# Value panels of a dilated attention as seven products for eight, and what moves with them

## The chip, the cores and the metric

The kernel runs on one core of a Trainium2 chip. The metric is device time in microseconds (us) of one execution, as the median of several runs. A core has five engines with their own instruction streams: TensorE (PE in the rows) multiplies matrices, VectorE (DVE) and ScalarE (ACT) work element by element, GpSimd (POOL) here adds weight blocks and starts transfers, SyncE (SP) starts transfers. They meet only at semaphores. Matrix products land in PSUM, eight banks of 128 x 512 f32; everything else lies in SBUF (in the rows: "arena").

## The reference

Two layers of a mixer (mLSTM branch, dilated attention branch, gates) and a swiglu MLP, then a windowed attention block and a gated linear attention block, for 256 tokens of width 1024, in f32. What the change touches is the value part of `qkv_a` and the order around it:

```python
def mixer(u, w_in, ...):
    z = u @ w_in
    qk_m, v_m, o_m, gate_m, qkv_a, gates_br = jnp.split(z, idx, axis=-1)
    y_a = mlstm_branch(qk_m, v_m, o_m, gate_m, ...) @ w_a
    y_b = dilated_attention(qkv_a, slopes) @ w_b
    g_a, g_b = jnp.split(gates_br, 2, axis=-1)
    return (jax.nn.sigmoid(g_a) * y_a + jax.nn.sigmoid(g_b) * y_b) @ w_out

def dilated_attention(qkv, slopes):          # three patterns, 8 slots, heads of 64
    ...
    for g, (win, dil) in enumerate(ATT_PATTERNS):
        o, lse = banded_attention(q[g], k[g], v[g], slopes[g], dil, win // (2 * dil))
    w = jax.nn.softmax(jnp.stack(lses, axis=0), axis=0)
    return (w[..., None] * jnp.stack(outs, axis=0)).sum(0)

# modulation, once a layer, from the vector c:
    ada = c_act @ w_ada[l] + b_ada[l]
    sh1, sc1, g1, sh2, sc2, g2 = jnp.split(ada, 6, axis=-1)
```

## The kernel before

The kernel is written by hand, engine by engine: one long function for TensorE, one for VectorE, one for ScalarE, one for GpSimd, each of which writes its instructions in the order in which they run. Semaphores order them across engines; a wait holds everything that stands behind it on that engine. The two layers run from 0 to about 640 us and on to about 1260 us, the two later blocks after that.

Weights come in panels of 512 columns (two panels make a group of 1024 x 512) into a ring of seven, loaded from SP. A layer's part that matters here runs so:

- Twelve query and key tiles ("AQK 0" to "AQK 11"), with pieces of the mLSTM between them, the minis. Behind some minis VectorE does a *modulation turn* (`beside_mix`): it multiplies one transferred part of `w_ada` by the vector c, with two scalar_tensor_tensor operations of 128x1028, or four where two vectors are to be served (a double turn; in layer 1 from its fifth turn on). The table `MINI_TURNS` says behind which minis. POOL starts the transfer for a later turn when a turn frees one of two slots.
- "HT 3", four transposes of the last mLSTM head, and then the value tiles "VA 0" to "VA 5", two for each of three patterns: 128 tokens x 512 columns, eight matmuls each. ScalarE copies them to SBUF.
- Scores, softmax, transposes and weighted sums of the dilated attention, by pairs of slots (`scores(u)`, `turned(u)`, `values(u)`, u = 0 to 3). A pair has two heads with two score tiles each: "SC 4 1" is head 4, tokens 128 to 255. VectorE drains both tiles of a head (with the distance bias), takes the row maximum and scales it, and goes on to the next head; ScalarE makes the exponentials; VectorE divides ("probs n").
- Between these, the gate products "GA p0", "GB p0", later "GA p1", "GB p1": a 1024-wide panel group times the tokens, made of seven products instead of eight. POOL makes two sums of weight blocks for each (`gate_weight_sums`), VectorE two more ("w6", "w3"), and the products are added up by VectorE from PSUM. They run in the order 1, 2, 4, 5, 7, 6, 3; product 6 needs w6.
- "WA 0", "WA 1", "WB 0", "WB 1", the output projections of both branches; VectorE multiplies each by its gate ("WB 0 drained"), adds ("mix 0"), and does turns between them, by the table in the loop. Then the second half with GA p1 and GB p1.

PSUM banks are taken in turn: `open_tile` hands out the next of eight, and the first matmul into it waits until its last tenant is drained. So the order of tiles decides whose drain a tile waits for.

In the rows one instruction of a helper has the helper's line: L598 and L600 are the transposes and matmuls, L2240, L2243 and L2246 VectorE's tensor_tensor, tensor_scalar and scalar_tensor_tensor, L2836 its maximum, L3455 and L3457 POOL's gate sums, L3439 and L3441 its sums for the MLP, L3470 and L3472 those of the last block, L3502 its transfers.

Of the kernel before, what the change touches and what calls it, by code (L numbers as in the profile page):

```python
# [265 lines left out]
def program(nc, a, out, marks):  # L266
    with ExitStack() as ctx:
# [19 lines left out]
        gate_sums_made = sem("gate_sums_made")  # L287
        mlp_sums_made = sem("mlp_sums_made")
# [222 lines left out]
        UP = [(name, p) for p in range(5) for name in ("W1", "W3")]  # L511

# [66 lines left out]
        def _(pe):  # L579
# [143 lines left out]
            for l in range(DEPTH):  # L723
# [86 lines left out]
                def va(j, w):  # L810

                    g, tt = j // 2, j % 2
                    ps = open_tile(f"VA {j}")
                    for i in range(KD):
                        x = UT[:, i, tt * P:tt * P + P]
                        if g:
                            x = by_residue(UT[:, i, :])[:, tt, :]
                        mm(ps[:, :PW], x, w[i][:, :PW], start=(i == 0), stop=(i == KD - 1),
                           done=f"VA {j}" if i == KD - 1 else None)

                def scores(u):
# [4 lines left out]
                    for tt in range(NT):  # L826
# [20 lines left out]
                def values(u):  # L847

                    if u == 0:
                        for j in range(6):  # L850
                            pe.wait_ge(act_done, AC.at(f"VA {j} drained"))
# [686 lines left out]
        def _(act):  # L1538
# [99 lines left out]
            for l in range(DEPTH):  # L1638
# [73 lines left out]
                def va(n):  # L1712

                    act.wait_ge(pe_done, PE.at(f"VA {n} full"))
                    drain(f"VA {n}", VA[:, n % 2, PW * (n // 2):PW * (n // 2) + PW]).then_inc(
                        act_done, AC.drained(f"VA {n}"))

                def exponentials_of(u):

                    for n in (2 * u, 2 * u + 1):  # L1720
# [40 lines left out]
                va(0)  # L1761
                exponentials_of(0)
                va(1)
                va(2)
                turned(0)
                exponentials_of(1)
                va(3)
                va(4)
                va(5)
# [465 lines left out]
        def _(dve):  # L2235
# [474 lines left out]
            for l in range(DEPTH):  # L2710
# [113 lines left out]
                token_sums("gates", up_x, [gate_tokens[i] for i in (5, 6, 4)], False, gate_tokens[7])  # L2824
                for u in range(SLOTS // 2):
                    for n in (2 * u, 2 * u + 1):
# [3 lines left out]
                        for tt in range(NT):  # L2830
# [8 lines left out]
                            dve_done, DV.step(f"slot negmax {n}"))  # L2839
                    for n in (2 * u, 2 * u + 1):  # L2840
# [3 lines left out]
                        for tt in range(NT):  # L2844
                            ts(SC[n % 2][:, tt, :], SC[n % 2][:, tt, :], att[:, n % 2, 3, tt:tt + 1], None, ALU.mult).then_inc(
                                dve_done, DV.step(f"probs {n}" if tt else None))
                    if u >= 2:
                        gate_panel(0, u - 2)
                    beside_mix(1)
                for p in range(2):  # L2850
# [11 lines left out]
                    for n in range(2):  # L2862
# [9 lines left out]
                        beside_mix(((0, 0, 0, 0), (1, 0, 0, 1))[l][j])  # L2872
# [547 lines left out]
        def _(pool):  # L3420
# [22 lines left out]
            def gate_weight_sums(l, p, b):  # L3443
# [133 lines left out]
```

## Time and profile before

| | us |
|---|---|
| median of 3 runs | 2267.65 (2266.7 to 2269.16) |
| profiled execution | 2266.64 |
| its span | 2264.8 |
| TensorE busy | 2229.2 (98%) |
| VectorE busy | 1430.7 (63%) |
| ScalarE busy | 488.7 (22%) |
| GpSimd busy | 287.4 (13%) |

The span is what the trace covers, from the first to the last instruction. A busy share is a mean over stages of different kinds; what a stage waits for is read in that stage. Each f32 matmul of the program is two rows in the trace, and a row's end is modelled, so the pace of TensorE is read from start to start. A turn of VectorE shows as scalar_tensor_tensor rows of 128x1028 with short accumulator reads between.

### The profile page before, as it was taken

Reading aid. Unit: us, or ns where it says so; the run is one execution under the profiler, and the core shown is the slowest. Engines: PE = TensorE matmul, PEld = TensorE weight load, DVE = VectorE, ACT = ScalarE, POOL = GpSimd, SP = SyncE. Lnnn points to the kernel's source line nnn. Section 1 sums busy time; section 2 is a strip of 40 time slices with the busy share of each in tenths; the row PEclk is TensorE's granted clock in tenths of the full one; section 3 lists DMA queues with packets and bytes.
Section 4 is the critical chain, followed back from the end, with each engine's and each line's share of the span. In section 5 each row is a group of like instructions: output and inputs, shape, how many; then the busy total and the mean of one; then the engine's idle time right before and its main releaser. Section 6 shows DMA issues by size and latency. Waiting matters only on the chain.

```text
span 2264.8 us, 30050 instructions
## 1 busy us (share of the span) xinstructions
PE 2229.2 (98%) x12022; PEld 1820.3 (80%) x12022; DVE 1430.7 (63%) x2592; ACT 488.7 (22%) x1067; POOL 287.4 (13%) x181
## 2 busy tenths in 40 slices
PE   7999999999999999999999999999999999999998
PEld 5888598799868885988998655588888887768987
DVE  5676453645656566756656777775576468766655
ACT  1212230110012223201010365422200023343300
POOL 0000121331000001223310000000000001001442
PEclk9999999999999999999999999999999999999999
DMA  9885546444576655465655411433433324445542
GB/s 393 295 315 190 190 164 220 170 154 168 198 279 188 230 186 205 172 219 196 185 196 177 168 38 39 158 113 130 154 132 124 121 94 168 131 168 186 179 166 84
DMA packets 179770, 398.77 MB, mean 176 GB/s; under 512 B 21168, under 2 KB 25648, under 8 KB 176560
## 3 DMA queue, kind: packets, MB, share of 16 engines
q1 hardware_dynamic: 136736, 285.03, 35.8%
q0 software_dynamic: 24080, 93.69, 12.0%
q10 hardware_dynamic: 18816, 18.12, 2.5%
q8 instruction: 97, 1.59, 0.3%
q14 instruction: 41, 0.34, 0.0%
HBM read 395.71 MB, written 1.11 MB: 175 GB/s over the span
## 4 chain that ended last, share of the span: by engine, by line
PE 94%; DVE 4%; ACT 1%; issue 0%; DMA 0%; POOL 0%; DVEq 0%; SPq 0%; ACTq 0%
PE bank L600 91%; PE bank L598 3%; DVE arena L2240 2%; DVE arena L2246 1%; ACT arena L1540 1%; DVE arena L2243 0%; DVE junk L2246 0%; DMA arena<-in_x 0%; ACT L1540 0%; ACT arena L1543 0%; DVE arena L2836 0%; POOL arena L3470 0%; POOL arena L3472 0%; DVE arena L3236 0%; DVE arena L2305 0%
## 5 line engine op out<-in xcount | busy, mean ns | idle before, releaser
L600 PE MATMUL bank<-arena 128*128 128x256 f32 (+4 forms) x11438 | 2169.1, 357 | 12.9 <-DVE arena L2246 3.7
L600 PEld LDWEIGHTS bank<-arena 128*128 128x128 f32 (+2 forms) x11438 | 1754.2, 189 | 407.3 <-issue 225.0
L2240 DVE TENSOR_TENSOR arena<-arena 128x1024 f32<-128x1024 f32 (+6 forms) x567 | 475.6, 854 | 206.1 <-PE bank L600 172.7
L1540 ACT ACTIVATE arena<-arena 128x512 f32<-128x512 f32 (+5 forms) x443 | 222.6, 525 | 796.5 <-DVE arena L2240 471.0
L2246 DVE SCALAR_TENSOR_TENSOR arena<-arena 128x1028 f32<-128x1028 f32 (+6 forms) x367 | 314.3, 873 | 83.2 <-DMA arena<-in_w_ada 60.3
L2240 DVE TENSOR_TENSOR arena<-arena,bank 128x256 f32<-128x256 f32 (+2 forms) x382 | 171.6, 474 | 185.0 <-PE bank L600 173.9
L3502 POOL DMA_DIRECT2D arena<-in_w_ada x88 | 62.9, 715 | 1447.5 <-DVEq L2255 1404.4
L1540 ACT ACTIVATE arena<-bank 128x256 f32<-128x256 f32 (+1 forms) x129 | 53.0, 429 | 558.5 <-PE bank L600 557.8
L2240 DVE TENSOR_TENSOR arena<-bank,arena 128x512 f32<-128x512 f32 (+2 forms) x95 | 60.4, 646 | 155.6 <-PE bank L600 140.4
L1543 ACT ACTIVATE arena<-bank 128x512 f32<-128x512 f32 (+1 forms) x163 | 88.5, 600 | 310.6 <-PE bank L600 272.4
L2246 DVE SCALAR_TENSOR_TENSOR arena<-bank,arena 128x254 f32<-128x254 f32 (+2 forms) x184 | 78.0, 468 | 57.9 <-PE bank L598 28.2
L2243 DVE TENSOR_SCALAR arena<-arena 128x512 f32<-128x512 f32 (+6 forms) x258 | 83.3, 352 | 20.1 <-ACT arena L1540 13.6
L598 PEld LDWEIGHTS bank<-arena 128*128 128x128 f32 x584 | 68.0, 143 | 27.2 <-issue 20.4
L598 PE MATMUL bank<-arena 128*128 128x128 f32 x584 | 74.6, 276 | 13.1 <-DVE arena L2243 11.1
L2246 DVE SCALAR_TENSOR_TENSOR junk<-arena 128x1028 bf16<-128x1028 f32 x64 | 79.7, 1245 | 5.7 <-DMA arena<-in_w_ada 1.5
L1540 ACT ACTIVATE arena<-bank,arena 128x128 f32<-128x128 f32 (+2 forms) x138 | 57.5, 484 | 99.9 <-DVE arena L2243 32.9
L3439 POOL TENSOR_TENSOR arena<-arena 128x1024 f32<-128x1024 f32 x20 | 49.3, 2466 | 180.2 <-DMA arena<-in_w 80.8
L2243 DVE TENSOR_SCALAR arena<-bank,arena 128x256 f32<-128x256 f32 (+1 forms) x112 | 46.3, 467 | 30.4 <-PE bank L598 14.1
L1540 ACT ACT_TABLE_LOAD x48 | 61.6, 1283 | 4.2 <-PE bank L600 2.2
L2246 DVE SCALAR_TENSOR_TENSOR arena<-arena,bank 128x512 f32<-128x512 f32 (+1 forms) x40 | 24.5, 643 | 43.5 <-PE bank L600 42.7
L3441 POOL TENSOR_TENSOR arena<-arena 128x1024 f32<-128x1024 f32 x20 | 51.2, 2562 | 1.6
L3470 POOL TENSOR_TENSOR arena<-arena 128x1024 f32<-128x1024 f32 x14 | 35.4, 2527 | 87.0 <-PE bank L600 73.1
(39 smaller groups left out, 260.5 us busy)
## 6 DMA issues: line engine op xcount, KB each, us to landing
arena<-in_w_ada POOLq DMA_DIRECT2D x88, 1028.0 KB, 5.8
arena<-in_w_in SPq DMA_DIRECT2D x84, 1024.0 KB, 7.6
arena<-in_w SPq DMA_DIRECT2D x56, 1024.0 KB, 6.9
arena<-in_w_mlp_in SPq DMA_DIRECT2D x32, 1024.0 KB, 7.3
arena<-in_w_mlp_out SPq DMA_DIRECT2D x32, 1024.0 KB, 6.9
arena<-in_w_gla SPq DMA_DIRECT2D x12, 1024.0 KB, 6.9
arena<-in_w_ada SPq DMA_DIRECT2D x16, 514.0 KB, 19.4
arena<-in_w_a SPq DMA_DIRECT2D x8, 1024.0 KB, 7.2
```

The costliest lines, as they stand in the source:

```text
L598: ins = nc.tensor.transpose(out, lhsT, rhs)
L600: ins = nc.tensor.matmul(out, lhsT, rhs, start=start, stop=stop)
L1540: return nc.scalar.activation(out, x, f, **kw)
L1543: return nc.scalar.activation(out, tile(key)[:, :out.free_size()], f)
L2240: return V.tensor_tensor(out, x, y, op)
L2243: return V.tensor_scalar(out, x, s1, s2, op0, op1) if op1 is not None else V.tensor_scalar(out, x, s1, None, op0)
L2246: return V.scalar_tensor_tensor(out=out, in0=x, scalar=s, in1=y, op0=op0, op1=op1, **kw)
L3439: nc.gpsimd.tensor_tensor(up_sum(at), a21, a22, ALU.add).then_inc(up_sums_made, 1)
L3441: nc.gpsimd.tensor_tensor(a21, a11, a21, ALU.subtract).then_inc(up_sums_made, 1)
L3470: nc.gpsimd.tensor_tensor(wsum, a21, a22, ALU.add).then_inc(mlp_sums_made, 1)
L3502: pool.dma_start(adaw[:, n % ADA_SLOTS], half_source(job, q)).then_inc(ada_in[n % ADA_SLOTS], 16)
```

## The change

The value tiles of a pattern become seven products of 512 x 256 blocks, like those of the gates: "VA g 1" to "VA g 7" for pattern g, each four matmuls (k = 0 to 3) of 256 columns. Pattern 0 uses the token sums that the gates have; patterns 1 and 2 use sums of strided tokens ("classes"), which VectorE makes once a layer. POOL makes two sums for each value panel (`value_panel_sums`), VectorE w6 and w3 and seven additions from PSUM, ScalarE one copy instead of two drains.

The order moves too. On TensorE the first two products of pattern 0 stand ahead of the scores of pair 0, four of pattern 1 ahead of `turned(0)` with its last three behind, product 3 of pattern 1 goes into a given bank; the first half of the scores of pair 2 stands ahead of `values(0)`, the second behind `turned(1)`. The modulation turns move from pairs 0 to 2 into the minis and to WB 0 (layer 0) and WB 1 (layer 1). POOL's first two gate sums wait for "probs 3" and "probs 5", and the later ones stand two jobs (GA p1) and one job (GB p1) later. The gates' token sums stand ahead of the last mini.

```diff
-MINI_TURNS = (2, 4, 6, 8, 9, 11)
+MINI_TURNS = (1, 2, 3, 4, 5, 6, 8, 9)
-GATE_JOBS = {21: [(0, 0, 0)], 22: [(0, 0, 1)], 23: [(0, 1, 0)], 25: [(0, 1, 1)],
-             45: [(1, 0, 0)], 46: [(1, 0, 1)], 47: [(1, 1, 0)], 49: [(1, 1, 1)]}
+GATE_JOBS = {22: [(0, 0, 0), (0, 0, 1)], 25: [(0, 1, 0)], 26: [(0, 1, 1)],
+             46: [(1, 0, 0), (1, 0, 1)], 49: [(1, 1, 0)], 50: [(1, 1, 1)]}
+VALUE_JOBS = {22: [(0, g) for g in range(NPAT)], 46: [(1, g) for g in range(NPAT)]}
...
+                def value_products(g, order, over=None):
+                    q = quarters(value_panel_at(l, g))
+                    x, sums, tag = value_tokens(g)
+                    ops = {1: (q[0], x[0]), 2: (q[1], x[2]), 4: (q[3], sums[4]), 5: (gate_sum, sums[5]),
+                           7: (q[2], sums[7]), 6: (q[0], sums[6]), 3: (q[1], x[3])}
+                    for i in order:
+                        key = f"VA {g} {i}"
+                        ps = open_tile(key, marks.get((Progress.phase, "bank", over), 0) if over and i == 3 else None)
...
+                        for k in range(KH):
+                            mm(ps[:, :2 * P], ops[i][1][:, k, :], ops[i][0][:, k, :], start=(k == 0), stop=(k == KH - 1),
+                               done=key if k == KH - 1 else None)
...
-                va(0, w)
+                value_products(0, ORDER[:2])
                 scores(0)
-                va(1, w)
+                value_products(0, ORDER[2:])
                 release(w)
                 w = panel()
-                va(2, w)
+                value_products(1, ORDER[:4])
                 turned(0)
+                value_products(1, (6, 7, 3), "PT 1 1")
+                release(w)
                 scores(1)
-                va(3, w)
+                w = panel()
+                value_products(2, (1, 2, 4, 5, 6, 7, 3))
                 release(w)
-                w = panel()
-                va(4, w)
-                va(5, w)
-                release(w)
+                scores(2, (0,))
+                values(0)
                 turned(1)
-                values(0)
-                scores(2)
+                scores(2, (1,))
                 w = panel()
                 gate_products(0, 0, ORDER[:4])
...
                 for n in range(12):
+                    if n == 11:
+                        token_sums("gates", up_x, [gate_tokens[i] for i in (5, 6, 4)], False, gate_tokens[7])
...
+                def value_weight_sums(g):
+                    dve.wait_ge(value_sums_made, values_made(l, g, 7))
+                    panel_sums(f"VA {g}", value_panel_at(l, g), 6, f"VA {g} 1", gate_sum)
+                    panel_sums(f"VA {g}", value_panel_at(l, g), 3, f"VA {g} 2")
...
-                    beside_mix(1)
+                    if u == 3:
+                        beside_mix(1)
...
-                        beside_mix(((0, 0, 0, 0), (1, 0, 0, 1))[l][j])
+                        beside_mix(((1, 0, 0, 0), (1, 1, 0, 1))[l][j])
...
+                if p == 0:
+                    pool.wait_ge(dve_of[f"layer {l}"], DV.of(f"layer {l}", f"probs {3 + 2 * b}"))
...
+            def value_panel_sums(l, g):
+                n = value_panel_at(l, g)
+                a11, a12, a21, a22 = quarters(n)
...
+                nc.gpsimd.tensor_tensor(gate_sum, a21, a22, ALU.add).then_inc(value_sums_made, 1)
+                pool.wait_ge(value_sums_made, values_made(l, g, 5))
+                nc.gpsimd.tensor_tensor(a21, a11, a21, ALU.subtract).then_inc(value_sums_made, 1)
```

On TensorE, at the first gate product of layer 0: before, the last rows of `scores(2)` ("SC 4 1" in bank3, "SC 5 1" in bank4) and "GA p0 1" behind them.

```order
L600 MATMUL bank3<-arena 128x256 [waits act_done layer 0]
L600 MATMUL bank4<-arena 128x256
L600 MATMUL bank3<-arena 128x128
L600 MATMUL bank4<-arena 128x128
L600 MATMUL bank5<-arena 128x128 [waits act_done layer 0,panel0_in,panel6_in]
```

And after: "SC 4 0" (bank2) and "SC 5 0" (bank3) stand ahead of `values(0)` (bank4) and of four transposes, then come "SC 4 1" (bank1) and "SC 5 1" (bank2), and "GA p0 1".

```order
L621 MATMUL bank2<-arena 128x256 [waits act_done layer 0,dve_done layer 0]
L621 MATMUL bank3<-arena 128x256
L621 MATMUL bank4<-arena 64x256 [waits act_done layer 0,dve_done layer 0]
L619 MATMUL bank5<-arena 128x128 [waits dve_done layer 0]
L621 MATMUL bank1<-arena 128x256 [waits dve_done layer 0]
L621 MATMUL bank2<-arena 128x256
L621 MATMUL bank3<-arena 128x128 [waits dve_done layer 0,panel0_in,panel6_in]
```

The first gate product went into a bank that ScalarE had drained (a transpose); now it goes into that of "SC 5 0", which VectorE drains.

On VectorE, in layer 1 between WB 0 and the weight sums w6 and w3 of GA p1 (128x4x256), before:

```order
L2240 TENSOR_TENSOR arena<-bank0,arena 128x512
L2240 TENSOR_TENSOR arena<-arena 128x512
L2246 SCALAR_TENSOR_TENSOR junk,arena<-arena 128x1028
L2246 SCALAR_TENSOR_TENSOR arena<-arena 128x1028
L2240 TENSOR_TENSOR arena<-bank1,arena 128x512
L2240 TENSOR_TENSOR arena<-arena 128x512
L2240 TENSOR_TENSOR arena<-arena 128x4x256 x2
```

After, from WB 1's product on (the rows of WB 0 and its turn stand ahead of it as before):

```order
L2267 TENSOR_TENSOR arena<-bank5,arena 128x512
L2267 TENSOR_TENSOR arena<-arena 128x512
L2273 SCALAR_TENSOR_TENSOR junk,arena<-arena 128x1028
L2273 SCALAR_TENSOR_TENSOR arena<-arena 128x1028
L2273 SCALAR_TENSOR_TENSOR junk,arena<-arena 128x1028
L2273 SCALAR_TENSOR_TENSOR arena<-arena 128x1028
L2267 TENSOR_TENSOR arena<-arena 128x4x256 x2
```

A double turn stands between WB 1's add and the weight sums.

On POOL, in layer 1 (three pairs of sums: GB p0, GA p1, GB p1; the transfers between them are for turns), before:

```order
L3455 TENSOR_TENSOR arena<-arena 128x1024 [waits pe_done layer 1,dve_done layer 1,panel6_in,panel5_in]
L3457 TENSOR_TENSOR arena<-arena 128x4x256 [waits gate_sums_made]
L3502 DMA arena<-in_w_ada 128x2x1028 [waits ada_free]
L3455 TENSOR_TENSOR arena<-arena 128x1024 [waits pe_done layer 1,dve_done layer 1,panel4_in,panel3_in]
L3457 TENSOR_TENSOR arena<-arena 128x4x256 [waits gate_sums_made]
L3502 DMA arena<-in_w_ada 128x2x1028 [waits ada_free] x2
```

After:

```order
L3515 TENSOR_TENSOR arena<-arena 128x1024 [waits pe_done layer 1,dve_done layer 1,panel6_in,panel5_in]
L3517 TENSOR_TENSOR arena<-arena 128x4x256 [waits gate_sums_made]
L3579 DMA arena<-in_w_ada 128x2x1028 [waits ada_free] x3
L3515 TENSOR_TENSOR arena<-arena 128x1024 [waits pe_done layer 1,dve_done layer 1,panel4_in,panel3_in]
L3517 TENSOR_TENSOR arena<-arena 128x4x256 [waits gate_sums_made]
L3579 DMA arena<-in_w_ada 128x2x1028 [waits ada_free]
```

The sums of GA p1 stand behind three transfers that wait for turns, where one stood ahead of them.

## Rows read from the trace of the kernel before

**Rows 1.** The page, its first part: busy us, share, instructions.

```profile
PE 2229.2 (98%) x12022; PEld 1820.3 (80%) x12022; DVE 1430.7 (63%) x2592; ACT 488.7 (22%) x1067; POOL 287.4 (13%) x181
```

**Rows 2.** TensorE's waits, first of the list: us in total, times, the longest.

```profile
PE bank L598 <- DVE arena L2243: 11.1, 3, 10.4
```

**Rows 3.** Timeline of TensorE: start, us, operation, count, [idle before]; two value tiles, AQK.

```profile
268.42 13.90 PE L600 MATMUL bank<-arena 128*128 128x512 f32 x32
282.16 0.27 PE L598 MATMUL bank<-arena 128*128 128x128 f32 x1
...
837.67 9.47 PE L600 MATMUL bank<-arena 128*128 128x256 f32 x43
846.98 0.60 PE L598 MATMUL bank<-arena 128*128 128x128 f32 x4
```

**Rows 4.** VectorE's operations by shape, 234.89 to 345; two stretches of all engines.

```profile
L2240 DVE TENSOR_TENSOR arena<-arena,bank 128x256 f32<-128x256 f32 x14 | 5.5, 418 | 5.7 <-PE bank L600 5.4
L2240 DVE TENSOR_TENSOR arena<-arena 128x1024 f32<-128x1024 f32 x4 | 4.9, 1221 | 0.2
L2240 DVE TENSOR_TENSOR arena<-arena 128x512 f32<-128x512 f32 x5 | 3.4, 692 | 0.2
...
234.89:342.00 107.11, 107.11 (x656) 78.17 (x655) 60.14 (x109) 31.14 (x68) 20.49 (x12) 1.00 0.50 179
847.42:955.00 107.58, 107.02 (x655) 77.96 (x654) 76.43 (x133) 31.02 (x68) 20.52 (x12) 1.00 0.50 171
```

**Rows 5.** Timeline of VectorE behind "SC 4 1", layer 0.

```profile
288.18 0.69 DVE L2246 SCALAR_TENSOR_TENSOR arena<-arena,bank 128x512 f32<-128x512 f32 x1 [0.35 <-PE bank L600]
...
290.24 1.29 DVE L2246 SCALAR_TENSOR_TENSOR arena<-arena,bank 128x512 f32<-128x512 f32 x2
```

**Rows 6.** Timeline of TensorE at "GB p0 6", layer 1: idle before in brackets.

```profile
931.00 2.25 PE L600 MATMUL bank<-arena 128*128 128x128 f32 x18 [0.56 <-DVE arena L2240]
```

**Rows 7.** Timeline of VectorE, the last mini of layer 1.

```profile
840.25 0.76 DVE L2615 BATCH_NORM_STATS2 arena<-bank 128x6 f32<-128x256 f32 x2 [3.05 <-PE bank L600]
...
842.39 0.99 DVE L2243 TENSOR_SCALAR arena<-bank,arena 128x256 f32<-128x256 f32 x2
```

**Rows 8.** Timeline of VectorE: a small operation, beside a POOL sum (L3439) from 393.43.

```profile
393.45 2.35 DVE L2243 TENSOR_SCALAR arena<-arena 128x8 f32<-128x8 f32 x1
```

**Rows 9.** Timelines, layer 1: VectorE from WA 1's turn on, then TensorE at "GA p1 6".

```profile
958.33 0.08 DVE L2246 DVE_READ_ACCUMULATOR arena<-arena 128x1 f32 x1
...
960.14 1.23 DVE L2246 SCALAR_TENSOR_TENSOR junk<-arena 128x1028 bf16<-128x1028 f32 x1
...
965.41 0.69 DVE L2240 TENSOR_TENSOR arena<-bank,arena 128x512 f32<-128x512 f32 x1 [0.21 <-DVE arena L2246]
966.13 3.16 DVE L2240 TENSOR_TENSOR arena<-arena 128x512 f32<-128x512 f32 x3
...
968.22 16.24 PE L600 MATMUL bank<-arena 128*128 128x128 f32 x144
```

**Rows 10.** Timelines: POOL in layer 1, then POOL and VectorE side by side.

```profile
951.75 0.71 POOL L3502 DMA_DIRECT2D arena<-in_w_ada  x1 [8.91 <-DVEq L2255]
...
2091.05 3.37 POOL L3470 TENSOR_TENSOR arena<-arena 128x1024 f32<-128x1024 f32 x1 [1.43 <-DVE arena L2240]
...
2092.12 3.39 DVE L2246 SCALAR_TENSOR_TENSOR arena<-arena 128x1028 f32<-128x1028 f32 x1
2095.44 3.37 DVE L2246 SCALAR_TENSOR_TENSOR arena<-arena 128x1028 f32<-128x1028 f32 x1
```

**Rows 11.** Stretches (us, TensorE busy (rows), granted clock, DMA), and two pauses.

```profile
1855.20:1858.70 3.50, 3.50 (x11) 0.51 0.98 368
...
1854.75 7.54 PE L600 MATMUL bank<-arena 128*128 128x256 f32 x26 [1.25 <-ACT arena L1540]
...
2017.17 2.18 PE L600 MATMUL bank<-arena 128*128 128x256 f32 x9 [2.48 <-DVE arena L2246]
2014.00:2020.00 6.00, 3.50 (x15) 1.00 0.50 172
```

More of the change, by code:

```diff
@@ L511, in program, with value_panel_at, values_made, value_tokens @@
         UP = [(name, p) for p in range(5) for name in ("W1", "W3")]
+        def value_panel_at(l, g):
+            return gate_first[l] - 6 + 2 * g
+        def values_made(l, g, i):
+            return 2 * (NPAT * l + g) + (1 if i == 5 else 2)
+        class_x = [UT[:, KH * j:KH * j + KH, r::RES] for j in range(2) for r in range(RES)]
+        class_tokens = {i: area(M["WORK"] + KH * P * j, KH, P) for j, i in enumerate((5, 6, 7, 4))}
+        def value_tokens(g):
+            return (class_x, class_tokens, "classes") if g else (up_x, gate_tokens, "gates")
+        def value_blocks(g):
+            return {(i, m): VA[:, m - 1, PW * g + 2 * P * (i - 1):PW * g + 2 * P * i] for i in (1, 2) for m in (1, 2)}
         spare_sum = area(M["SIG"] + 1024, KH, 2 * P)
@@ L809, in _, with scores @@
                     release(w)
[L810 to L821, printed above, removed]
+                def value_products(g, order, over=None):
[6 more added lines that the diff above has]
+                        ps = open_tile(key, marks.get((Progress.phase, "bank", over), 0) if over and i == 3 else None)
+                        if i in (4, 5, 6, 7):
+                            pe.wait_ge(dve_done, DV.at(f"{tag} x{i}"))
+                        if i in (6, 3):
+                            pe.wait_ge(dve_done, DV.at(f"VA {g} w{i}"))
+                        if i in (5, 7):
+                            pe.wait_ge(value_sums_made, values_made(l, g, i))
+                        for k in range(KH):
+                            mm(ps[:, :2 * P], ops[i][1][:, k, :], ops[i][0][:, k, :], start=(k == 0), stop=(k == KH - 1),
+                               done=key if k == KH - 1 else None)
+                def scores(u, tts=range(NT)):
                     if u == 0:
@@ L825, in scores @@
                             pe.wait_ge(act_done, AC.at(f"AQK {n} drained"))
-                    for tt in range(NT):
+                    for tt in tts:
                         keys = [f"SC {2 * u + e} {tt}" for e in range(2)]
@@ L849, in values @@
                     if u == 0:
-                        for j in range(6):
-                            pe.wait_ge(act_done, AC.at(f"VA {j} drained"))
+                        for g in range(NPAT):
+                            pe.wait_ge(dve_done, DV.at(f"VA {g} c12"))
                     for n in (2 * u, 2 * u + 1):
@@ L1711, in _, with first_value, exponentials_of @@
                         act_mini(h, s)
[L1712 to L1720, printed above, removed]
+                def first_value(g):
+                    act.wait_ge(pe_done, PE.at(f"VA {g} 1 full"))
+                    func(value_blocks(g)[1, 2], tile(f"VA {g} 1")[:, :2 * P], ACT.Copy).then_inc(
+                        act_done, AC.drained(f"VA {g} 1"))
+                def exponentials_of(u, heads=(0, 1)):
+                    for n in [2 * u + e for e in heads]:
                         act.wait_ge(dve_done, DV.at(f"slot negmax {n}"))
@@ L2839, in _ @@
                             dve_done, DV.step(f"slot negmax {n}"))
+                    if u == 0:
+                        for _ in product_sums("VA 0", value_blocks(0), value_read(0)):
+                            pass
+                    if u == 1:
+                        value_weight_sums(2)
+                        first_sum("VA 2", value_blocks(2), value_read(2))
                     for n in (2 * u, 2 * u + 1):
@@ L3457, in gate_weight_sums @@
                 nc.gpsimd.tensor_tensor(a21, a11, a21, ALU.subtract).then_inc(gate_sums_made, 1)
+            def value_panel_sums(l, g):
+                n = value_panel_at(l, g)
+                a11, a12, a21, a22 = quarters(n)
+                for m in (n, n + 1):
+                    pool.wait_ge(panel_in[m % RING], 16 * (m // RING + 1))
+                if g:
+                    pool.wait_ge(pe_of[f"layer {l}"], PE.of(f"layer {l}", f"VA {g - 1} 5 full"))
+                    pool.wait_ge(dve_of[f"layer {l}"], DV.of(f"layer {l}", f"VA {g - 1} w6"))
+                else:
+                    pool.wait_ge(pe_of[f"layer {l}"], PE.of(f"layer {l}", "S 3 full"))
+                nc.gpsimd.tensor_tensor(gate_sum, a21, a22, ALU.add).then_inc(value_sums_made, 1)
+                pool.wait_ge(value_sums_made, values_made(l, g, 5))
+                nc.gpsimd.tensor_tensor(a21, a11, a21, ALU.subtract).then_inc(value_sums_made, 1)
             def mlp_sums():
@@ L3492, in _ @@
                     value_sums((n - 74) // 4)
+                for job_ in VALUE_JOBS.get(n, ()):
+                    value_panel_sums(*job_)
                 for job_ in GATE_JOBS.get(n, ()):
```

31 lines of the change are left out of this document (22 added, 9 removed).

## The prediction

> **What bounds the kernel now.** I read the page first: TensorE is busy 98% of a span of 2264.8 us, DVE 63%, ACT 22%, POOL 13% [rows 1]. So the reader is to see that time is gained only by taking work from TensorE, and lost wherever another engine makes it wait. The list of its waits comes second: the longest is the one at the start, 10.4 us [rows 2]. TensorE hardly waits today, so a forecast is a sum of removed TensorE work and of new waits. Therefore I then read, stage by stage, how early each thing that TensorE needs is ready: the margin, not the share.
>
> The profiled execution took 2266.64 us, 1.84 more than its span; the median of the three runs is 2267.65. I make the sum against 2266.64 and add 1.0 at the end.
>
> **TensorE work removed.** A value tile has 16 rows of 512 columns in the trace (two for each matmul). Two tiles run from 268.42 to 282.16: 6.87 each [rows 3], 41.2 for six. The new products are 21 a layer, 8 rows of 256 columns each. Such rows go at (846.98 - 837.67) / 43 = 0.2166 us [rows 3]: 1.73 a product, 36.4 for 21. That is -4.8, which is seven for eight and a little more for the narrower rows; four of the old tiles also follow work of another kind and lose a little at their start, so I take the eighth, **-5.1 us a layer, -10.3 in both**, between 9.6 and 10.3.
>
> **What is added beside TensorE.** Per layer DVE gets six weight sums (1.22 each), 21 adds from PSUM (0.42 each) and four class sums (0.69) [rows 4]: 18.9 us. It is busy 60.1 of 107.1 us in layer 0's stretch and 76.4 of 107.6 in layer 1's [rows 4], and there loses three turns of 2.4 or 5.1. ACT drops six drains for three copies. POOL gets six sums of 2.36. None of these engines becomes the bound; I cost them at nothing except where their order makes TensorE late, the four places below. The new wait of POOL's first two gate sums for the probabilities has, queued behind it, the transfer that is released by pair 3's turn, which comes later anyway; TensorE wants those sums only at the fifth products of GA p0 and GB p0, several products later: nothing. SP's panel loads follow the releases, which move by under 6 us beside a ring of seven panels: nothing. The eight mini turns of layer 0 are single (two operations of 1.23 [rows 9]), and with them the margin that term 3 works out for layer 1 (3.05 + 3.6) holds a whole turn and the token sums: nothing. The sum of value panel 2 ends two adds (0.84) behind its last product, and "AV 0" needs it with the first scores of pair 2 between: 0 to 0.8, I take 0.
>
> **1. A bank behind a reduction.** Splitting the scores of pair 2 shifts the banks: "GA p0 1" now opens the bank of "SC 5 0". DVE drains that only after both tiles of head 4, its maximum and its scaling. From the row of before: the second drain of head 4 starts at 288.18, its maximum and scaling follow, and the first drain of head 5 starts at 290.24 and, as half of a row of two, ends at 290.9 [rows 5]. "GA p0 1" comes right behind those scores on TensorE, at about 288.1. The drain order is fixed and there is nothing else between, so TensorE waits 2.9 us, in each layer: **+5.8**. Two smaller bank waits of the same kind (0.1 each) make +0.4 in both layers.
>
> **2. A wait that goes.** In layer 1 "GB p0 6" waited 0.56 us for a weight sum queued behind the double turn of pair 2 [rows 6]. That turn is gone: **-0.6**.
>
> **3. The last mini of layer 1.** From the fifth mini turn on, turns of layer 1 are double (5.1 us, not 2.4). Before, DVE had been idle 3.05 us when the last head's chain began at 840.25, and TensorE took its result at 846.98, 3.6 after the chain's end [rows 3, 7]. The change puts a second half turn (2.6) and the token sums (4 x 0.69) ahead: 2.4 late, 1.2 left. But now POOL makes the first value panel's sums there, and small DVE operations beside a POOL sum are held: one of 128x8 took 2.35 us [rows 8]. Two holds less the 1.2 are 3.5, and without any it is nothing; I take the middle, **+1.8**.
>
> **4. The gate weights of layer 1's second half.** This is the largest term. DVE runs from WA 1's turn straight through WB 0, a turn (960.14 to 965.2), WB 1 (965.41), its add and the weight sum w6, which ends at 966.13 + 0.69 + 1.22 = 968.0 [rows 9]. "GA p1 6" starts at 968.22 and needs it [rows 9]: 0.2 us of margin. The change puts one more double turn between the add and w6. A turn takes 965.41 - 960.14 = 5.27 with its gaps [rows 9], so TensorE waits **5.0 us** there. Nothing covers it: the sixth product is the next on TensorE, and all DVE work ahead is in order.
> To that comes POOL. The sums of GA p1 now stand two jobs later on POOL, behind the transfer that WA 1's turn releases (before, 951.75 was WA 0's) [rows 10]. That turn ends at 958.4 [rows 9], the issue takes 0.7 [rows 10], so they start at about 959.5, beside the turn behind WB 0. Where POOL sums lie beside such scalar_tensor_tensor operations the two alternate: at 2092.12 and 2095.44 these took 3.39 and 3.37 us, not 1.23, beside a POOL sum that took 3.37 [rows 9, 10]. Two holds are **+4.3**. The bounds are 0 and 4.3; as both sums fall into one unbroken run of these operations I take the upper. In layer 0 the turns are single (2.4) and the same two effects, about 2.6 and 4.3, stay inside the time to "GA p1 6" by some 1 us.
> The Trainium skill (SBUF — State Buffer, section "SBUF: two separate sides") says why: GpSimd and a VectorE operation with two SBUF inputs share a port pair that is an exclusive lock, and the loser waits a whole instruction. That speaks against placing sums beside turns, and the trace agrees (3.39 for 1.23); without it the fourth term would be 5.0, and the sum 4.3 lower.
>
> **5. The clock.** Granted clock is 1.00 nearly throughout, but 0.51 from 1855.2 to 1858.7, behind a pause of 1.25 us [rows 11]. In 3.5 us at half speed about 1.7 is lost. After the pause of 2.48 at 2017 it did not fall [rows 11]. The change makes three pauses of 2.9, 2.9 and 9.3 us. I count one fall for the long one and half a fall for the two short: **+2.6**, between 0 and 5.1.
>
> **The sum.** -10.3 + 5.8 + 0.4 - 0.6 + 1.8 + 9.3 + 2.6 = +9.0: 2266.64 + 9.0 = 2275.6, and with the 1.0 to the median 2276.6.
>
> **Rivals.**
> A, faster: the weight sum w6 of GA p1 is in time. That is one mechanism at one place, term 4: if DVE reached WB 0 some 5 us sooner than TensorE's order lets it, the added turn would lie in idle time. Then -10.3 + 6.2 - 0.6 = -4.7, 2262.9, and if the bank waits went as well, 2256.7. It decides below a wait of 0.2 us at "GA p1 6". For it: DVE as a whole has 37% free [rows 1]. Against it: that chain begins with WA 1's product, so it can't begin sooner, and its margin is 0.2 us [rows 9].
> B, gain and waits cancel: banks 6.2 and the extra turn 5.0, but POOL's sums fall where DVE does no such work, the last mini keeps its margin and the clock holds: -10.3 + 6.2 - 0.6 + 5.0 = +0.3, 2267.9. This is also the case if the layer 1 turn ran into slack partly and the clock fell once.
> C, the clock at every pause: three falls (5.1) and the mini's upper bound: 2276.6 + 2.5 + 1.7 = 2280.8. It decides if pauses of 2.9 us behind small matmuls suffice; the 1.25 us case speaks for, the 2.48 us case against.
> The Trainium skill (TensorE: Matmul & The Clock Gate, "Part 1: The HAM clock gate") holds that half rate is the default and that activity alone lifts it, judged by a monitor that runs free of the program. By it each fall depends on where a pause lies, as the two rows at 1855 and 2017 also suggest, and C would be the upper end.
> That the products are not made as seven can't be: the order of the change has 21 of them a layer.
>
> **Chances.** My forecast, with one or two falls: 0.45. C: 0.13. B and what lies between it and the forecast under 2272: 0.25. A and A with the bank waits: 0.17. This measurement can tell about 0.2%, 4.5 us, from no change. So faster (under 2263.1) 0.17, same 0.25, slower (over 2272.2) 0.58. The range leaves out the work alone and a little above C: 2262.5 to 2281.
>
> **What would show it.** In the new trace: value products at 1.73 us each, 5.1 less in the stretch per layer; TensorE idle 2.9 us ahead of "GA p0 1" in both layers, ended by DVE's scalar_tensor_tensor; no wait at "GB p0 6"; in layer 1 a wait of 9 us at "GA p1 6" ended by a DVE tensor_tensor, with scalar_tensor_tensor rows of 3.4 beside POOL rows of 3.3; granted clock near 0.5 for some 3.5 us behind it. I am wrong in the size if POOL's sums lie ahead of that turn (4.3 less), in the sign if the wait at "GA p1 6" is under 1 us.

## The result and the profile after

The changed kernel takes 2282.53 us in the median of four executions (2280.89 to 2282.8), the kernel before 2267.58: a ratio of 1.0063, with an interval of 1.0051 to 1.0075. That is slower by 15 us, as to the sign forecast, and 1.5 us outside the stated range (2262.5 to 2281). The profiled execution took 2282.69 with a span of 2280.9, 16.05 more than that of before.

TensorE's waits, longest first (us in total, times, the longest), which answers to [rows 2]:

```profile
PE bank L619 <- DVE arena L2270: 12.9, 4, 10.7
PE bank L621 <- DVE arena L2267: 12.6, 5, 9.5
PE bank L621 <- DVE arena L2273: 9.5, 4, 2.9
```

The longest wait is as old as the kernel (10.7 at the start); the 9.5 and the 2.9 are new. The timeline of TensorE at the four places of the forecast, with the idle time ahead in brackets:

```profile
269.00 8.80 PE L621 MATMUL bank<-arena 128*128 128x256 f32 x40
...
286.71 10.47 PE L621 MATMUL bank<-arena 128*128 128x128 f32 x80 [2.89 <-DVE arena L2273]
850.61 0.66 PE L619 MATMUL bank<-arena 128*128 128x128 f32 x4 [1.53 <-DVE arena L2270]
902.68 4.59 PE L621 MATMUL bank<-arena 128*128 128x128 f32 x25 [2.89 <-DVE arena L2273]
980.71 4.48 PE L621 MATMUL bank<-arena 128*128 128x128 f32 x22 [9.54 <-DVE arena L2267]
```

The first row is five value products of pattern 2, 40 rows, which end where the scores begin at 277.73: 1.75 each, the joint at their end included. Then "GA p0 1" of layer 0, "HT 3" and "GA p0 1" of layer 1, and "GA p1 6". Ahead of the first pause VectorE does what [rows 5] showed, one drain and the maximum ahead of the drain that TensorE waits for:

```profile
283.82 0.69 DVE L2273 SCALAR_TENSOR_TENSOR arena<-arena,bank 128x512 f32<-128x512 f32 x1 [1.30 <-PE bank L621]
284.54 1.22 DVE L2878 TENSOR_REDUCE arena<-arena 128x2 f32<-128x1024 f32 x1
285.80 0.17 DVE L2270 TENSOR_SCALAR arena<-arena 128x2 f32<-128x2 f32 x1
285.88 1.29 DVE L2273 SCALAR_TENSOR_TENSOR arena<-arena,bank 128x512 f32<-128x512 f32 x2
```

At GA p1 the timelines of VectorE and POOL, which answer to [rows 9, 10]:

```profile
961.41 0.69 DVE L2267 TENSOR_TENSOR arena<-bank,arena 128x512 f32<-128x512 f32 x1 [0.21 <-DVE arena L2273]
962.14 3.07 DVE L2267 TENSOR_TENSOR arena<-arena 128x512 f32<-128x512 f32 x1
965.31 3.19 DVE L2273 SCALAR_TENSOR_TENSOR junk<-arena 128x1028 bf16<-128x1028 f32 x1
...
973.27 0.69 DVE L2267 TENSOR_TENSOR arena<-arena 128x512 f32<-128x512 f32 x1
974.07 1.23 DVE L2273 SCALAR_TENSOR_TENSOR junk<-arena 128x1028 bf16<-128x1028 f32 x1
...
979.33 2.56 DVE L2267 TENSOR_TENSOR arena<-arena 128x1024 f32<-128x1024 f32 x2 [0.21 <-DVE arena L2273]
962.29 2.36 POOL L3515 TENSOR_TENSOR arena<-arena 128x1024 f32<-128x1024 f32 x1
964.73 2.69 POOL L3517 TENSOR_TENSOR arena<-arena 128x1024 f32<-128x1024 f32 x1
```

POOL starts at 962.29 and holds the add of WB 0 (3.07 for 0.69) and the first operation of the turn (3.19 for 1.23). WB 1's add ends at 974.0; the added turn takes until 979.1, and only then come w6 and w3. TensorE had been ready since 971.

The granted clock, by stretches (us, TensorE busy (rows), granted clock, DMA, GB/s), which answers to [rows 11]:

```profile
288.10:291.60 3.50, 3.50 (x19) 0.51 0.00 0
690.90:694.30 3.40, 3.40 (x9) 0.50 0.20 25
902.50:906.00 3.50, 3.32 (x16) 0.51 0.00 0
971.00:984.50 13.50, 3.96 (x20) 0.62 0.23 80
1855.00:1870.00 15.00, 13.31 (x69) 1.00 0.63 211
1991.30:1994.80 3.50, 3.37 (x8) 0.51 0.46 177
2032.30:2035.80 3.50, 3.50 (x10) 0.51 0.00 0
```

At 0.5 the clock is at the lower of its two levels, 1.2 GHz. It fell in or right behind each of the three new long pauses, and at three other places (691, 1991, 2032) where it had not in the trace of before; where it fell in that one beyond 1850 (1855) it did not. Both have one more near 76.

### The profile page after: what moved, and what is told of

The parts are those of the page before. It is cut to its first block, busy times and chain, and to the rows that moved or that the text cites. A ratio compares the mean times of both kernels' runs of the same rounds, so it can differ in the third digit from the quotient of the medians.

```text
span 2280.9 us, 30488 instructions
## 1 busy us (share of the span) xinstructions
PE 2227.3 (98%) x12166; PEld 1853.2 (81%) x12166; DVE 1480.5 (65%) x2654; ACT 484.1 (21%) x1061; POOL 312.2 (14%) x193
## 4 chain that ended last, share of the span: by engine, by line
PE 88%; DVE 8%; DMA 1%; ACT 1%; issue 1%; POOL 0%; SPq 0%; DVEq 0%; ACTq 0%
PE bank L621 86%; DVE arena L2273 3%; PE bank L619 3%; DVE arena L2267 2%; DMA arena<-in_w_ada 1%; DVE junk L2273 1%; ACT arena L1569 1%; DVE arena L2270 1%; ACT L1569 0%; ACT arena L1572 0%; DVE arena L2609 0%; DVE arena L2878 0%; POOL arena L3545 0%; POOL arena L3547 0%; DVE arena L3293 0%
## 5 line engine op out<-in xcount | busy, mean ns | idle before, releaser
L621 PE MATMUL bank<-arena 128*128 128x256 f32 (+5 forms) x11582 | 2166.6, 355 | 29.0 <-DVE arena L2267 12.6
L621 PEld LDWEIGHTS bank<-arena 128*128 128x128 f32 (+2 forms) x11582 | 1787.4, 189 | 389.6 <-issue 189.4
L2267 DVE TENSOR_TENSOR arena<-arena 128x1024 f32<-128x1024 f32 (+7 forms) x587 | 506.1, 877 | 203.4 <-PE bank L621 172.2
L2267 DVE TENSOR_TENSOR arena<-arena,bank 128x256 f32<-128x256 f32 (+2 forms) x424 | 188.3, 469 | 206.5 <-PE bank L621 194.2
L1572 ACT ACTIVATE arena<-bank 128x512 f32<-128x512 f32 (+1 forms) x151 | 81.5, 599 | 264.9 <-PE bank L621 213.9
```

The lines of the kernel that those rows point to most:

```text
L621: ins = nc.tensor.matmul(out, lhsT, rhs, start=start, stop=stop)
L1572: return nc.scalar.activation(out, tile(key)[:, :out.free_size()], f)
L2267: return V.tensor_tensor(out, x, y, op)
```

## The experiments

The runs were made on several chips. Beside e1 to e4 the kernel before took 2268.45 us (median of 22 executions, 2266.72 to 2272.77), beside b1, b2, a_again and e5_mini 2268.74, beside c1 and e6 2267.85; beside b3, b_again, a_shift and e5_again one execution took 2266.82.

### e1_bank: a bank skipped ahead of GA p0 1

```diff
                 scores(2, (1,))
+                st["next"] = (st["next"] + 1) % 8
                 w = panel()
                 gate_products(0, 0, ORDER[:4])
```

> The changed kernel with one bank skipped ahead of GA p0 1, in both layers, so that this product opens the bank of AV 0 (drained by ScalarE) and not that of SC 5 0. Theory (the wait is VectorE's drain behind the maximum of head 4, and the clock falls because of the pause): both waits of 2.9 us at GA p0 1 go and with them the two falls of the clock right behind them, 1.6 us each; -9 us against the changed kernel's 2282.5: 2273.5. Rival (VectorE is late as a whole there, so the next product waits in its place): a wait of 2 to 3 us moves to GA p0 2 to 6, 2279 to 2282.5. Rival on the clock (it falls there without a pause): the waits go but the falls stay, 2276.7.

Measured: 2273.4 us, ratio 1.0018 (1.0009 to 1.0028). TensorE has no idle time between 280 and 296, nor between 892 and 904, and the clock falls at neither place. TensorE's list of waits now reads:

```profile
PE bank L621 <- DVE arena L2268: 12.6, 5, 9.5
PE bank L621 <- DVE arena L2274: 3.7, 2, 2.5
```

The row for scalar_tensor_tensor is back at the 3.7 of before, and the 9.5 stands. The drain behind the maximum was the cause, and 9 us is its price with the clock, against the changed kernel's median; single executions of e1 lie between 2270.76 and 2275.92.

### e2_sums and e3_turn: the two parts of the wait at GA p1 6

e2 makes the sums sooner:

```diff
-             46: [(1, 0, 0), (1, 0, 1)], 49: [(1, 1, 0)], 50: [(1, 1, 1)]}
+             46: [(1, 0, 0), (1, 0, 1), (1, 1, 0)], 50: [(1, 1, 1)]}
```

> The changed kernel with POOL's sums of GA p1 in layer 1 made right behind those of GB p0 (three jobs sooner), so that they no longer lie beside the turn behind WB 0. Theory (the wait of 9.5 us at GA p1 6 is one added double turn, 5.2, and two holds by POOL sums, 4.3): the wait falls to 5.2; 2278.2. Rival (it is all the turn and what VectorE has queued; sums and turn merely share the time): the wait stays at 9 to 9.5 and the time at 2282.5. The clock should still fall behind it, since 5 us of pause are left.

e3 moves the added turn from WB 1 to WA 2 in layer 1:

```diff
-                        beside_mix((1, 1, 0, 0)[j])
+                        beside_mix(((1, 1, 0, 0), (1, 1, 1, 0))[l][j])
...
-                        beside_mix(((1, 0, 0, 0), (1, 1, 0, 1))[l][j])
+                        beside_mix(((1, 0, 0, 0), (1, 0, 0, 1))[l][j])
```

> The changed kernel with the added turn of layer 1 behind WA 2 in place of WB 1; the sums of GA p1 stay beside the turn of WB 0. Theory: the wait at GA p1 6 falls from 9.5 to about 4.1 (two holds of 2.1 to 2.2 less 0.2 of margin) and the turn behind WA 2 costs nothing, since VectorE has some 10 us of TensorE's WA and WB products to catch up: 2277.1. Rival (the turn is late wherever it stands in this stretch): a new wait of 2 to 5 us at the output projection, 2280 to 2282.

Measured: e2 2278.97 us (six executions, 2274.42 to 2282.48), ratio 1.0043 (1.0029 to 1.0057); e3 2276.67 (ten, 2270.14 to 2282.09), ratio 1.003 (1.002 to 1.0041). With such a spread the waits, not the times, tell the two parts apart. The row of TensorE at "GA p1 6", of e2 and then of e3:

```profile
978.54 11.67 PE L621 MATMUL bank<-arena 128*128 128x128 f32 x77 [5.19 <-DVE arena L2267]
```

```profile
976.32 13.94 PE L621 MATMUL bank<-arena 128*128 128x128 f32 x97 [4.08 <-DVE arena L2267]
```

5.19 is the turn and 4.08 the two holds, each less the margin of 0.2; 9.54 is both together, less the margin once. In e3 the held operations stand as in the changed kernel:

```profile
963.21 3.08 DVE L2267 TENSOR_TENSOR arena<-arena 128x512 f32<-128x512 f32 x1
966.39 3.19 DVE L2273 SCALAR_TENSOR_TENSOR junk<-arena 128x1028 bf16<-128x1028 f32 x1
```

The rival for e2, that only the turn counts, falls; so does that for e3, since no new wait stands behind WA 2.

### e4_all: the three edits together

> The three edits together: bank skipped, sums of GA p1 early, turn behind WA 2. Theory: no wait at GA p0 1 and none at GA p1 6 (margin 0.2 as in the kernel before), so no fall of the clock at these three places: -9.0 - 9.5 - 1.8 = -20.3, 2262.2, give or take 1.7 for a fall of the clock elsewhere; this is 5 us below the kernel before. Rival (the two holds and the turn overlap, so single edits take away less than their sum, or the value products bring less than 4.6 a layer): 2267 to 2272.

Measured: 2260.61 us, ratio 0.9964 (0.995 to 0.9978), so faster than the kernel before. "GA p1 6" follows product 7 without a gap, as does "GA p0 1" the scores. The value products do bring their gain once nothing waits behind them. The only new wait left in the two layers is "HT 3" of layer 1, 1.54.

### b1_bank: the bank wait alone, in the kernel before

```diff
-                        ps = open_tile(f"{key} {i}")
+                        ps = open_tile(f"{key} {i}", marks[Progress.phase, "bank", "SC 5 0"] if (p, b, i) == (0, 0, 1) and (Progress.phase, "bank", "SC 5 0") in marks else None)
```

> The kernel before, with one thing of the change alone: GA p0 1 opens the bank of SC 5 0 (in both layers), which VectorE drains behind the maximum of head 4. No value products, no moved turn. Theory: a wait of 2.9 us at GA p0 1 in both layers and behind each a fall of the granted clock that costs 1.6: +9.0 against the kernel before (2268.5 on that chip, 2267.6 on the first): about 2277. Rival (a pause of 2.9 us costs itself alone, and the falls in the changed kernel came from the sum of several waits): +5.8, 2274. Rival (the wait is the value work's, VectorE being late from that): under +2.

Measured: 2279.97 us, ratio 1.0049 (1.0034 to 1.0064), 11.2 more than before where 9.0 was expected. TensorE's two rows at "GA p0 1", then the clock behind them and at one more place:

```profile
291.89 8.28 PE L600 MATMUL bank<-arena 128*128 128x128 f32 x47 [2.89 <-DVE arena L2246]
911.84 6.33 PE L600 MATMUL bank<-arena 128*128 128x128 f32 x40 [2.90 <-DVE arena L2246]
...
290.90:297.80 6.90, 5.91 (x28) 0.51 0.01 2
697.10:700.50 3.40, 3.40 (x10) 0.50 0.34 77
912.10:915.50 3.40, 3.40 (x18) 0.51 0.00 0
```

The waits are 2.9 without any value product, so they belong to the bank alone. The clock fell behind both, in layer 0 for twice as long, and at 697, where this kernel does what the kernel before does (at 76 and 1868 too). The rivals, that a pause of 2.9 costs itself alone or that VectorE is late from the value work, are out.

### c1_fill: TensorE at work through the long wait

```diff
+                        if (l, p, b, i) == (1, 1, 0, 6):
+                            for _ in range(5):
+                                for e in range(2):
+                                    for k in range(KH):
+                                        mm(ps[:, e * P:e * P + P], ops[7][0][:, k, e * P:e * P + P], ops[7][1][:, k, :],
+                                           start=(k == 0), stop=(k == KH - 1))
                         if i in (6, 3):
                             pe.wait_ge(dve_done, DV.at(f"{key} w{i}"))
```

> The changed kernel with TensorE kept at work while it waits for the weight sum at GA p1 6 in layer 1: product 7 of GA p1 is made five times more into the bank of product 6, which overwrites it (8.9 us of work, no result of it is used). It measures the clock's part of that wait by itself. Theory (the clock falls because TensorE stands still): the idle time shrinks from 9.5 to under 1 us, the granted clock stays at 1.00 there, GA p1 6 starts as late as before, and the product behind it runs at full pace: 1.8 less than the changed kernel, whose executions lie at 2281 to 2285: 2280.7 from 2282.5. Rival (the fall comes from where in time the place lies, or from VectorE and POOL being busy): the clock falls all the same, and the time is unchanged.

Measured: 2277.55 us, ratio 1.004 (1.0025 to 1.0056). The stretch in c1 and in the changed kernel, in that order:

```profile
960.00:984.00 24.00, 23.49 (x208) 1.00 0.52 179
978.88 11.32 PE L621 MATMUL bank<-arena 128*128 128x128 f32 x99 [0.51 <-DVE arena L2273]
```

```profile
960.00:984.00 24.00, 14.46 (x106) 0.80 0.56 208
```

With TensorE at work the clock stays at 1.00, though the weight sum is as late as before. In each of the six traces that pause here (the changed kernel's three, e1, e2, e3) it fell. So the fall comes from TensorE's standing still, and not from the time or from the load of the other engines. Beside the kernel before, "GA p1 3" comes 9.6 us late in c1 where it came 11.4 late in the changed kernel: the 1.8 of the fall are gone, the wait is not. The whole time fell by 5, not 1.8: the trace of c1 has no fall at 76 and none at 1991 either, 1.7 each. That the other executions lack them too isn't shown.

### b2_shift, b3_shift2, a_again, b_again, a_shift, e5_again: where else the clock falls

Six single executions, of kernels unaltered or moved in time by more matmuls at "AQK 0" of layer 0, whose result the tile's own sum overwrites (four in b2_shift and a_shift, eight in b3_shift2):

```diff
                 ps = open_tile(key)
+                if key == "AQK 0" and Progress.phase == "layer 0":
+                    for i in range(4):
+                        mm(ps[:, :T], w[i][:, cols + 2 * n * P:cols + (2 * n + 1) * P], x[:, i, :], start=(i == 0), stop=(i == 3))
```

> The kernel before, with four more matmuls of 128x256 in AQK 0 of layer 0 (their result is overwritten by the tile's own sum), so that all behind it lies 1.73 us later and nothing else changes. It asks whether the falls of the clock at places that the change does not touch come from where in time these places lie. Theory: TensorE's work grows by 1.7 us; the falls at 690 and beyond 1850 are others than in the kernel before (one at 1855), each present or absent, so that the time is 2268 + 1.7 plus 0 to 3.4. Rival (the value products or the waits cause them): the falls stay as they were, one at about 1857, and none near 692.

> The changed kernel once more, unaltered. Theory: the three waits of 2.9, 2.9 and 9.5 us stand again to 0.1 us with a fall of the clock behind each; of the falls at untouched places (690, 1991, 2032 in the first trace) some stand elsewhere or are missing, since only their cost of 1.7 us each varies from one execution to the next. Rival (they belong to the change as firmly as the others): the same list, within 1 us.

> The kernel before, unaltered, for one more list of the places where the clock falls. Theory (falls at untouched places belong to the single execution): their number differs from the first trace's (one, at 1855) by one or two, and each costs 1.7: 2266.6 plus 0 to 3.4. Rival (they are tied to the kernel): one fall at 1855 and none at 690 again.

> The kernel before with eight more matmuls of 128x256 in AQK 0 of layer 0, so that all behind it lies 3.5 us later. Theory: TensorE's work grows by 3.5; falls at untouched places again by chance. Rival (the fall at 691 is tied to bank waits, which this kernel has not): none near 694.

> The changed kernel with four more matmuls of 128x256 in AQK 0 of layer 0, 1.7 us later from there on. The falls behind the three pauses should stand again (about 290, 904, 976). Theory (chance): the one at 691 and those beyond 1850 may be missing or elsewhere. Rival (691 is tied to the bank waits): a fall at about 692 again.

> The best version so far (three edits and the last mini turn moved to the first mini), unaltered, for one more list. Theory: one to three falls, not the same as in its first trace (76, 2008); 2257 to 2261. Rival: the same two falls.

Measured, with the places (us) where the granted clock fell (one that every trace has in its last 10 us is left out); in bold those behind the new pauses:

| | us | falls |
|---|---|---|
| before, first trace | 2266.64 | 77, 1855 |
| b_again | 2269.86 | 76, 691 (twice as long) |
| b2_shift | 2267.86 | 75, 2017 |
| b3_shift2 | 2270.8 | 692, 2020 |
| changed, first trace | 2282.69 | 77, **288**, 691, **903**, **974**, 1991, 2032 |
| a_again | 2285.3 | 76, **287** (twice as long), 693, **905**, **977**, 1994, 2035 |
| a_shift | 2286.03 | 77, **288**, 691 (twice as long), **906**, **978**, 1995, 2036 |
| e5_again | 2264.52 | 75 and 686 (both twice as long), 1973, 2014 |

At the three new pauses it fell in every trace that has them. The other falls do not stand at changing places. In all 16 traces of this record they lie at five places of the program that the change leaves alone (besides, e1_bank and e4_all have one each at 17, and e6_mini one at its own pause of 3.98). Two of the five have no pause: near 76, and near 690 in layer 1, TensorE is busy throughout and has just done 32 rows of 16 columns; the clock fell in 11 of 16 traces at each. The other three are pauses as old as the kernel, of 1.25 us (a fall in 3 of 16 traces), 1.19 us (5) and 2.48 us (12). In the changed kernel's first trace they read:

```profile
1869.10 14.05 PE L621 MATMUL bank<-arena 128*128 128x256 f32 x64 [1.25 <-ACT arena L1569]
...
1991.43 10.94 PE L621 MATMUL bank<-arena 128*128 128x256 f32 x26 [1.19 <-DVE arena L2273]
...
2031.52 16.14 PE L621 MATMUL bank<-arena 128*128 128x256 f32 x54 [2.48 <-DVE arena L2273]
```

Two of them have a fall there (1991, 2032), and a_again has the same list:

```profile
693.40:696.80 3.40, 3.40 (x10) 0.51 0.26 48
1994.00:1997.30 3.30, 3.27 (x8) 0.50 0.59 237
2034.90:2038.30 3.40, 3.40 (x10) 0.50 0.00 0
```

So whether the clock falls at such a place differs between executions of one kernel, as the theory had it (the first trace of before against b_again), and a fall near 690 needs no bank wait (b_again, b3_shift2). But for the changed kernel the rivals came true: a_again repeats the first trace's list, 2 to 3 us later, and a_shift has its fall at 691. Its three traces have four such falls each, the four of the kernel before two each (shifted executions counted); and near 690 the clock fell in all seven traces that pause at "GA p0 1" and in four of the nine that do not. That these falls are pure chance, and that the change does not make them more frequent, isn't shown; what decides about them stays open.

Two of the six times missed what was expected: b2_shift lies below it (2267.86 for 2269.7 to 2273.1), e5_again above (2264.52 for 2257 to 2261), with four falls, two of them twice as long.

### e5_mini and e6_mini: the last wait in layer 1

e4 with another table of mini turns, and then with two turns behind the second mini:

```diff
-MINI_TURNS = (1, 2, 3, 4, 5, 6, 8, 9)
+MINI_TURNS = (0, 1, 2, 3, 4, 5, 6, 8)
```

> The three edits together (bank skipped, sums of GA p1 early, turn behind WA 2) and the last mini turn moved from the tenth mini to the first (table 0, 1, 2, 3, 4, 5, 6, 8). Theory: the chain of the last mLSTM head in layer 1 starts about 3 us sooner and POOL's first value sums are over before its small operations; the wait of 1.5 us at HT 3 goes: 2260.6 - 1.7 = 2258.9. Rival (double turns at the fifth to eighth turn hold up an earlier head): the wait moves to HT 1 or HT 2, 2260 to 2263.

```diff
-MINI_TURNS = (0, 1, 2, 3, 4, 5, 6, 8)
+MINI_TURNS = (0, 1, 1, 2, 3, 4, 6, 8)
...
-                    if n in MINI_TURNS:
-                        beside_mix(1)
+                    beside_mix(MINI_TURNS.count(n))
```

> The version with all edits, and the mini turns at 0, 1, 1, 2, 3, 4, 6, 8: two turns behind the second mini, where VectorE stood idle for 7 us, and none behind the sixth, where a double turn held up head 1 by 1.2 us. Theory: the wait of 1.2 us at HT 1 in layer 1 goes and none comes in its place: 2258.3 - 1.2 = 2257.1, 11 to 12 us below the kernel before on the same chip, with executions 1.7 or 3.4 higher where the clock falls. Rival (the two turns in a row meet a transfer that has not landed, since there are only two slots): a wait of 1 to 4 us at head 0 in either layer, 2259 to 2262.

Measured: e5 2258.26 us, ratio 0.9951 (0.9935 to 0.9968); e6 2266.33, ratio 0.9995 (0.9986 to 1.0003). In e5 the wait at "HT 3" is gone and one of 1.19 stands at "HT 1", so both sides had a part of it. That is 0.3 less waiting; that e5 is faster than e4 isn't shown, as their intervals overlap and e5_again took 2264.52. In e6 the rival came true, and its time lies 4 us above the rival's, which had no fall of the clock in it (there is one at 185, behind the longer wait): a second turn in a row waits for its transfer, and TensorE for the head behind it. First VectorE's turns in both layers, then TensorE's "HT 0" in both:

```profile
169.34 1.23 DVE L2274 SCALAR_TENSOR_TENSOR arena<-arena 128x1028 f32<-128x1028 f32 x1 [3.12 <-DMA arena<-in_w_ada]
778.81 1.23 DVE L2274 SCALAR_TENSOR_TENSOR arena<-arena 128x1028 f32<-128x1028 f32 x1 [3.06 <-DMA arena<-in_w_ada]
...
185.85 1.97 PE L619 MATMUL bank<-arena 128*128 128x128 f32 x8 [3.98 <-DVE arena L2271]
798.20 1.09 PE L619 MATMUL bank<-arena 128*128 128x128 f32 x8 [1.48 <-DVE arena L2271]
```

## Why the prediction was wrong, step by step

The direction and the numbers of four of the five terms were right, one of them partly by luck; the step that failed is **term 5, the clock**: forecast +2.6, measured +8.4. Against the first trace:

| step | forecast | trace |
|---|---|---|
| value work, small bank waits | -9.9 | -9.1 |
| 1. GA p0 1, two layers | +5.8 | +5.8 |
| 2. GB p0 6 | -0.6 | -0.7 |
| 3. minis of layer 1 | +1.8 | +1.9 |
| 4. GA p1 6 | +9.3 | +9.6 |
| 5. clock | +2.6 | +8.4 |
| sum | +9.0 | +16 |

The trace's column compares the start of the same tile in both traces; for the value work it is the time from "VA 0 1" (235.14) to "GA p0 1" (286.71) less the pause of 2.89, 48.68 us, against 53.22 from "VA 0" to "GA p0 1" before.

**The clock.** I counted one and a half falls of 1.7 for three pauses. All three fell: 1.6, 1.5 and 1.9, together 5.0. The pause of 2.48 at 2017 without a fall [rows 11] misled me: it was the exception, as 12 of the 16 traces have a fall there. b1_bank and c1_fill show that the pauses are the cause, and my upper bound of 5.1 held for them. With 5.0 for the clock and the other terms as measured, the sum would have been 2280.1, inside the range. What I put at nothing are falls at places that the change leaves alone: in the first trace +1.7 at 691 and +1.7 net beyond 1850. They differ between executions of one kernel (2266.64 and 2269.86 for the kernel before), and the range had no width for that. But I can't call the rest bad luck: the medians of four executions each differ by 15.0, 2.5 more than the measured terms with 5.0 for the clock, and the changed kernel's three traces all have these falls. Why stays open.

**The value work.** Inside a run of products the pace of 1.73 us was right, but the 21 took 36.9 us a layer, not 36.4. So 4.5 a layer was gained, not 5.1: there are more joints between work of unlike kinds now, where some 0.1 us is lost, as at the ends of VA's tiles before. The lower bound that I drew from the rows (4.8) was nearer than the value that I took.

**Term 1** was exact, 2.89 twice, and e1 and b1 show its cause from both sides. Rival A needed this wait or that at GA p1 6 to be absent, and fell.

**Term 3** came out right partly by luck: +1.8 was the middle between nothing and two holds, and the parts were others. The gates' token sums do not stand ahead of the last head's chain but behind it. The chain began 3.1 us late (843.38 for 840.25 [rows 7]), right behind a double turn, which is 1.0 more than TensorE's own delay there (849.08 for 846.98). And POOL held two of its small operations:

```profile
844.47 2.27 DVE L2270 TENSOR_SCALAR arena<-arena 128x2 f32<-128x2 f32 x1
...
847.03 2.10 DVE L2267 TENSOR_TENSOR arena<-arena 128x2 f32<-128x2 f32 x1
844.33 2.36 POOL L3530 TENSOR_TENSOR arena<-arena 128x1024 f32<-128x1024 f32 x1
846.77 2.35 POOL L3532 TENSOR_TENSOR arena<-arena 128x1024 f32<-128x1024 f32 x1
```

The holds cost 4.0; with the 1.0, and less the 3.6 that the result had in hand before, that is 1.4, beside a wait of 1.53.

**Term 4** was right in both parts, as e2 and e3 show one by one. The two held operations are the add and the first of the turn, not two of the turn. The lock that the Trainium skill describes (SBUF — State Buffer, "SBUF: two separate sides") fits both: add and turn read two operands from SBUF and were held (3.07 for 0.69). The estimate for layer 0 held: there is no wait at its "GA p1 6".

**Rivals.** B fell with POOL's holds. C, a fall at every pause, was nearest at 2280.8, and I gave it 0.13. The Trainium skill's rule beside it (TensorE: Matmul & The Clock Gate, "Part 1: The HAM clock gate"), that activity releases the clock, agrees with c1_fill's 1.00 against 0.80.

## What to carry to other kernels

Where TensorE is at 98%, a cheaper product is worth only what the margins of everything behind it allow: one of the three places that lost the gain had a margin of 0.2 us, the other two got a late bank by a shift of order, and three edits of order turned +15 into -8 without touching the products.
